# Forgetting attention with each head pair's query tiles in the order 0 1 6 7 2 3 4 5, page probabilities copied first in ScalarE's order, and the first decay rows in two transfers

## The reference, cut to what matters

```python
s = einsum(q_i, k) * 64 ** -0.5 + D[query] - D[key]      # D = cumsum(log f)
s = where(key position <= query position, s, -1e30)
p = softmax(s);  o = p @ v
```

## Time and profile before

| | us |
|---|---|
| median of three runs | 1789.3 |
| the profiled execution, as timed | 1788.96 |
| its span, first to last instruction | 1787.1 |
| forgetting attention, first instruction to the first of the next stage | 455.5 to 639.2 |

### The profile page before, as it was taken

The page is one execution under the profiler, slowest core; times in us unless marked ns, Lnnn a source line. Parts: engine busy times, 40 slices in busy tenths (PEclk is TensorE's granted clock), DMA queues, the critical chain, the costliest instruction groups (busy, mean ns, idle before and its releaser), DMA issues. The chain is left out here.

```text
span 1787.1 us, 27685 instructions
## 1 busy us (share of the span) xinstructions
PE 1568.5 (88%) x10583; PEld 1384.9 (77%) x10587; DVE 1030.4 (58%) x1718; ACT 624.8 (35%) x1112; POOL 744.3 (42%) x837
## 2 busy tenths in 40 slices
PE   4699989999688866999699559999999999699996
PEld 2467879999466645799587459999999999588874
DVE  1461009630455533555424596887777777669885
ACT  2432133231344442223223334443333442444352
POOL 1431014321000007775103469999999996000011
PEclk8899999999799987899699779999999999799998
DMA  8335532220421048422323202222222221885872
GB/s 328 113 138 166 189 108 81 80 87 15 142 63 31 29 140 224 105 84 76 118 104 94 69 24 85 73 79 79 73 73 73 88 83 70 256 292 176 278 243 93
DMA packets 136981, 211.00 MB, mean 118 GB/s; under 512 B 38756, under 2 KB 78484, under 8 KB 133522
## 3 DMA queue, kind: packets, MB, share of 16 engines
q1 hardware_dynamic: 134386, 200.32, 34.7%
q10 hardware_dynamic: 2464, 8.91, 1.3%
HBM read 166.16 MB, written 42.91 MB: 117 GB/s over the span
## 5 line engine op out<-in xcount | busy, mean ns | idle before, releaser
L2701 DVE SCALAR_TENSOR_TENSOR fu_tmp<-fu_zp,fu_cw,fu_tmp 128x1024 f32<-128x1024 f32 x88 | 150.9, 1714 | 75.9 <-ACT fu_tmp L2636 74.3
L2446 PE MATMUL fu_ps<-fu_thi,fu_wlo 128*128 128x272 f32 (+2 forms) x672 | 139.2, 288 | 0.0
L2446 PE MATMUL fu_ps<-fu_tlo,fu_whi 128*128 128x272 f32 (+2 forms) x672 | 138.9, 288 | 0.0
L2446 PE MATMUL fu_ps<-fu_thi,fu_whi 128*128 128x272 f32 (+2 forms) x672 | 138.9, 288 | 0.0
L3023 PE MATMUL fd_ps<-fd_bhi,fd_ahi 128*128 128x512 f32 x308 | 121.3, 394 | 19.2 <-DVE fd_blo L3134 19.2
L2478 POOL TENSOR_TENSOR fu_wlo<-fu_s,fu_whi 128x512 fp32r<-128x512 f32 x84 | 119.6, 1434 | 18.7 <-ACT fu_whi L2592 18.2
L2592 ACT ACTIVATE fu_whi<-fu_s 128x512 fp32r<-128x512 f32 x84 | 50.8, 628 | 216.1 <-PE fu_ps L2446 84.2
L3023 PE MATMUL fd_ps<-fd_blo,fd_ahi 128*128 128x512 f32 x308 | 121.1, 393 | 0.0
L3023 PE MATMUL fd_ps<-fd_bhi,fd_alo 128*128 128x512 f32 x308 | 121.1, 393 | 0.0
L2446 PE MATMUL fu_ps<-h_hi,fu_whi 128*128 128x272 f32 (+1 forms) x504 | 105.6, 291 | 15.4 <-POOL fu_wlo L2478 15.4
L2478 POOL TENSOR_TENSOR fu_wlo<-w_raw,fu_whi 128x512 fp32r<-128x512 f32 x67 | 109.8, 1640 | 9.7 <-ACT fu_whi L2592 9.7
(11 more groups left out here) (398 smaller groups left out, 4000.9 us busy)
## 6 DMA issues: line engine op xcount, KB each, us to landing
wa<-in_w_ada SPq DMA_DIRECT2D x24, 1024.0 KB, 5.6
w_raw<-in_w_up SPq DMA_DIRECT2D x88, 256.0 KB, 2.6
fd_b<-in_w_down SPq DMA_DIRECT2D x86, 256.0 KB, 3.7
fd_a<-scr_y SPq DMA_DIRECT2D x86, 256.0 KB, 3.7
scr_y<-fu_tmp SPq DMA_DIRECT2D x22, 544.0 KB, 4.5
fp_w<-in_w_fm SPq DMA_DIRECT2D x15, 512.0 KB, 3.4
scr_qkv<-fp_y SPq DMA_DIRECT2D x9, 512.0 KB, 2.9
dr_stg<-scr_qkv SPq DMA_DIRECT2D x8, 576.0 KB, 5.8
```

Source lines behind the costliest of these rows:

```text
L2446: last = pe.matmul(lane_of(q, o)[:, n, 0:size], w[:, o, kk], part(low, kk, slice(c, c + size)), start=(kk == 0 and m == 0), stop=(kk == HK ...
L2701: one = dve.scalar_tensor_tensor(yp, a, w, yp, ALU.mult, ALU.add)
```

## The change

A tuple `SPANS = (0, 3, 1, 2)` gives the order of tile pairs, and `tile_of(u)` takes the place of `u % NT` everywhere: a pair's tiles now come in the order 0 1, 6 7, 2 3, 4 5. ScalarE does `spread_c` at the head of its turn u, before `exp(u, 0)`, where it stood after the copies. `decays(0)` becomes four transfers, columns 0 to 255 of both rows with a semaphore of their own, then columns 256 to 1023 of both, and it is issued ahead of the table. Unit 0 waits for the first columns, unit 2 for the rest.

```diff
+        SPANS = (0, 3, 1, 2)
-        nb_in = [sem("fa_nb_in0"), sem("fa_nb_in1")]
+        nb_in, nb_first = [sem("fa_nb_in0"), sem("fa_nb_in1")], sem("fa_nb_first")
+        def tile_of(u):
+            return 2 * SPANS[u % NT // 2] + u % 2
...
         def output(eng, q, hh):
-            j, m = q // (NT // 2), q % (NT // 2)
+            j, m = q // (NT // 2), SPANS[q % (NT // 2)]
...
             def decays(j):
-                for hh in range(2):
-                    after(sp, max_set, 2 * NT * (j - 1))
-                    sp.dma_start(nb[:, j % 2, hh], K.scr_nd[2 * j + hh:2 * j + hh + 1].broadcast_to([P, SEQ])).then_inc(nb_in[j % 2], 16)
+                after(sp, max_set, 2 * NT * (j - 1))
+                for c in (slice(0, QC), slice(QC, SEQ)) if j == 0 else (slice(0, SEQ),):
+                    for hh in range(2):
+                        sp.dma_start(nb[:, j % 2, hh, c], K.scr_nd[2 * j + hh:2 * j + hh + 1, c].broadcast_to([P, c.stop - c.start]))\
+                            .then_inc(nb_first if c.stop == QC else nb_in[j % 2], 16)
...
+            decays(0)
             sp.dma_start(table[:], K.page_table).then_inc(table_in, 16)
-            decays(0)
             sp.wait_ge(table_in, 16)
             pages(0)
             decays(1)
...
             def scores(u):
-                j, i = u // NT, u % NT
+                j, i = u // NT, tile_of(u)
...
             for u in range(UNITS + 2):
+                if (u - FIRST) % 3 == 2 and 0 <= (u - FIRST) // 3 < NBATCH:
+                    spread_c((u - FIRST) // 3)
                 before = mine(u - 1, False) if 0 < u <= UNITS else []
...
                     for n in (before[:half], before[half:])[hh]:
                         spread(act, n)
-                if (u - FIRST) % 3 == 2 and 0 <= (u - FIRST) // 3 < NBATCH:
-                    spread_c((u - FIRST) // 3)
...
             def maximum(u, hh):
-                j, i = u // NT, u % NT
+                j, i = u // NT, tile_of(u)
                 n = (i + 1) * P
-                if i == 0:
+                if u == 0:
+                    dve.wait_ge(nb_first, 32)
+                if u == QC // P or u and u % NT == 0:
                     dve.wait_ge(nb_in[j % 2], 32 * (j // 2 + 1))
```

More of the change, by code:

```diff
@@ L1058, in forgetting_attention @@
             for hh in range(2):
-                for b in range(0, u % NT + 1, 4):
-                    groups.append((u, hh, b, min(4, u % NT + 1 - b)))
+                for b in range(0, tile_of(u) + 1, 4):
+                    groups.append((u, hh, b, min(4, tile_of(u) + 1 - b)))
         group_of = {g[:3]: n for n, g in enumerate(groups)}
@@ L1076, in spread @@
             u, hh, b, size = groups[n]
-            q, i = u // 2, u % NT
+            q, i = u // 2, tile_of(u)
             eng.wait_ge(t_mm, n + 1)
@@ L1234, in exp @@
             def exp(u, hh):
-                n = (u % NT + 1) * P
+                n = (tile_of(u) + 1) * P
                 act.wait_ge(max_set, 2 * u + hh + 1)
@@ L1290, in i_last @@
             def i_last(u):
-                return (u % NT) // 4 * 4
+                return tile_of(u) // 4 * 4
             def scale(u, hh):
```

## The result

The changed kernel takes 1780.55 us (median of 9 runs, 1775.64 to 1784.36) where the kernel before took 1791.4 us beside it (9 runs). The ratio is 0.9931, interval 0.991 to 0.9952: 12.3 us (9 to 16) of 1789.3, against the 12.7 forecast (1789.3 less 1776.6). The profiled execution was timed at 1777.7 us and its span is 1775.6 us, 11.5 less than before. Forgetting attention runs from 455.4 to 628.1 us: 172.7 us long instead of 183.7, so 11.0 of the 11.5 lie in this stage.

The account below looks back on a forecast made before the run. TensorE (88% busy) was taken to carry the kernel, held up by waits on ScalarE's copies and clock falls. Terms -2.0 - 7.4 - 6.3 + 3.1 = -12.6 us gave 1776.6 us, range 1770.5 to 1784.

Parts of the forecast that it names:

- part 3: Split first decay rows, table behind them: 2.85 us gained early, page 0 late; net +3.1 us, bounds -2.0 and +6.
- part 1: New tile order: shorter `turn` stalls, partly returned at new neighbours and before `turn_c(5)`; -2.0 us in sum.
- Part 2: `spread_c` first: copies lie in ScalarE's idle time, so waits before `values_c` go; -7.4 us, bounds -7.4 and -2.
- The clock: Low-clock time after the waits before `values_c` goes with them: -6.3 us, bounds 0 and -7.9.
- no difference: Rival: `spread_c` delays the exponentials (+5), page 0 late (+3), clock as before; 1788 to 1790 us, chance 0.08.
- the fall in part 3: Clock falls after the 3.9 us page wait before `scores_c(0)`: 5.5 us low, 2.5 us lost.
- The fall before `turn_c(5)`: The 2.0 us wait behind `scale_c` may bring a clock fall back; given half of 7 us x 0.46, 1.6 us.
- 6→7: Stall inside `turn` of tile 6 beside tile 7; claimed to stay in the new order.
- the next `turn` stall absorbs: Of the 2.5 us lost to low clock after the page wait, 1.1 us is absorbed by the following `turn` stall.
- page 0 in time: Rival: decay rows do not hold up the table; part 3 gives -2.0 instead of +3.1, 1771.5 us, chance 0.13.
- the clock falls all the same: Rival: waits of 1.66 to 2.0 us keep low-clock time as it was; 6.3 us lost, 1782.9 us, chance 0.22.
- Slower: Rival: after the page wait the clock stays low for the rest of the first pair; 1792 us, chance 0.05.

Follow-up runs that it names:

- e1: Kernel before with only `spread_c` moved to the head of ScalarE's turn: stage 170.0 us against 183.7, ratio 0.9888.
- e5: Changed kernel without the split decay transfers and with the table first; new order and `spread_c` first kept: stage 171.9 us, ratio 0.9927.
- e2: Kernel before with only the new tile order: stage 180.6 us against 183.7, ratio 0.9985.
- the four pairs above: Runs differing in tile order alone, all with `spread_c` first; new order longer: e5 less e1 +1.9 us, e4 less e6 +0.2, e10 less e11 +1.8, e7 less e12 +2.0.
- e4: Changed kernel with the table issued ahead of the four decay transfers: stage 168.0 us against 172.7, ratio 0.9882.
- e3: Kernel before with only the first decay rows split and the table issued behind them: stage 189.1 us against 183.7, ratio 1.002.
- e9: Changed kernel run again, unedited: stage 172.5 us, ratio to the kernel before 0.9905.
- e10: The changed kernel with the table first (e4) run again, unedited: stage 169.5 us, ratio 0.9922.
- e7: Changed kernel with the table first (e4), and VectorE's `scale_c` between the two maxima: stage 168.7 us, ratio 0.9906.
- e8: Changed kernel with the table issued between the first and second pair of decay transfers: stage 170.0 us, ratio 0.9911.
- e6: Changed kernel with the table first (e4), but tiles in the old order: stage 167.8 us, ratio 0.9915.
- e11: The old-order, table-first kernel (e6) run again, unedited: stage 167.7 us, ratio 0.991.
- e12: The old-order, table-first kernel (e6) with `scale_c` between the two maxima: stage 166.7 us, ratio 0.9917.

## Why the prediction was right

The time followed the likeliest case. The part that carries the gain, its mechanism and the times of the loads came out; the prices of the two small parts did not. Taken one after the other, the stage changes by -13.7 us with `spread_c` first (e1), +1.9 with the order added (e5) and +0.8 with part 3 (after). Forecast were -7.4 - 6.3 = -13.7, then -2.0 and +3.1. The last two are off by +3.9 and -2.3 us, and that they partly cancel is luck. So is the match of the first: the forecast's -13.7 holds 1.6 us for a fall of part 1, and e1 its late rise.

- **Part 2, -7.4 of waits.** Right: no wait on the copy is left, and e1 alone gives -13.7 us with the clock. ScalarE's idle time covers the copies; the 5 us of the rival "no difference" didn't come.
- **The clock, -6.3, and the fall in part 3, +2.5.** Net -3.8 was forecast for low-clock time. It went from 17.1 to 10.2 us, x 0.46 = -3.1. The first fall lasted 6.8 us, put at 5.5; 0.9 of it lies inside the page wait and costs nothing, so 5.9 are left, 0.2 us too many at 0.46. The fall before `turn_c(5)`, put down at one half of 7 us, came whole but half as long, in both profiles of the changed kernel: the same 1.6 us, by luck. It was put between "the 1.81 that did not and the 2.33 that did", but the third fall of before had followed a 1.43; the runs show no such threshold (last section).
- **Part 1, -2.0.** Alone it gives -3.1 (e2), beside `spread_c` first +0.2 to +2.0 (the four pairs above). The wait before `turn_c(5)` is 1.97 us (2.0 forecast). The `turn` stalls are 12.9 us in 12 waits, against 11.5 in 11. Timeline of the changed kernel, one stall of each kind that was missed:
```profile
486.30 2.02 PE L1173 MATMUL fa_psT<-fa_dg,fa_p 128*128 128x128 f32 x16 [0.27 <-ACT fa_pt L1090]
513.69 1.58 PE L1173 MATMUL fa_psT<-fa_dg,fa_p 128*128 128x128 f32 x12 [0.57 <-ACT fa_pt L1090]
531.56 1.80 PE L1173 MATMUL fa_psT<-fa_dg,fa_p 128*128 128x128 f32 x14 [1.89 <-ACT fa_pt L1090]
619.66 1.58 PE L1173 MATMUL fa_psT<-fa_dg,fa_p 128*128 128x128 f32 x12 [0.62 <-ACT fa_pt L1090]
```
  Of the 1.4 us, 0.6 is a stall that the sum had at nothing: the last tile of the stage, now tile 5, stalls although no unit follows it. 7→2 comes to 1.1 (0.27, 0.41, 0.41; 0.8 forecast) and 5→0 to 1.0 (0.57, 0.41; 0.7 forecast). 6→7 was carried over at its old 1.69 us ("6→7 stays"): it is 1.89 in unit 11, where `decay_c`, queued ahead of the maxima, lets VectorE start them 0.2 late. In unit 3 it would be 2.6 us (e4, e5), which the page wait hides. A stall depends on what the third engine has queued at that turn, not only on the two neighbouring tiles.
- **Part 3, +3.1.** The mechanism was right in its times: first maximum 458.99 (458.4 forecast), SyncE reads the table from 460.6 on (461.0), first page load 461.65 (462), page 0 complete by 469.98 (470.3). The wait is 2.91 us and not 3.9, mostly because TensorE arrived at 467.07 instead of 466.4; that is no gain, only the page was 0.3 early. The 1.1 us of the fall that "the next `turn` stall absorbs" weren't absorbed: TensorE was back at the higher clock in that `turn`, and the stall at 479.99 is a full 1.69. Two readings were wrong. Loads of 128 KB do stand in the trace of before (`tp_lng`, `tp_lnb`: 9.0 and 8.9 us to landing, and 3.0 for the pair here), and `gpre` was issued behind 3.0 MB, not 3.5. As a term of the sum, 3.1 is no single number: part 3 costs 5.4 us alone (e3), and 0.8 beside the other two (e5), because the long stall of unit 3 and a fall come without it too. Against the table issued first it costs 4.7 (e4) or 3.0 (e9 less e10). What the forecast called "the 2.85 gained are spent, and more" is shown by e4: with the table first the gain of the split stays and the page is in time.
- **The sum.** -12.6 was forecast in the profiled execution. The stage gives -11.0 and ends at 628.1 instead of 626.5; the stages behind it keep their length (1147.9 us before, 1147.5 after). Missing are 1.6. The `turn` stalls hold 1.4, the absorption that didn't come 1.1 and low clock 0.2; against them page 0 was 0.3 early and the waits for `scale_c` grew by 0.9 instead of 1.1. That makes 2.2; the difference of 0.6 is not placed.

Of the rivals, "page 0 in time" fell by the load's issue at 461.65, and "the clock falls all the same" by the 100 us at full clock from 477 on. It was no idle rival, though: e5 has 10.2 us of low clock without any page wait. "Slower" fell, as the fall behind the page wait was over by 477.

## What to carry to other kernels

A copy that another engine waits for belongs at the head of the helper engine's turn as soon as its input is ready; it costs nothing while the helper would be idle there, and in the profiled stage here it saved more by itself (13.7 us) than the whole change did (11.0). A tiny load on which other loads depend is issued ahead of large ones on the same queue (4.7 and 3.0 us of the stage here, not told apart in the whole time). When work is reordered between two engines, look at what a third has queued in each of the new places, and price a part both alone and beside the others.

## What the runs showed of the hardware

- The granted clock (1.2 or 2.4 GHz) falls behind short waits, in a way that one wait's length doesn't fix. In the profiles here, apart from the waits for `spread_c`: behind 2.6 us in unit 3 it fell in e2, e4, e5, e7 and e10, each time; behind the page waits of 2.8 to 3.9 us in the changed kernel, e9 and e3, each time; behind 1.97 us before `turn_c(5)` in the changed kernel, e9, e2, e5 and e8, but not in e4 and e10; behind 1.88 or 1.89 us in unit 11 in e5 and e8, but not in the changed kernel, e4, e7, e9 and e10. In e1, e6, e11 and e12, whose waits behind the rise are 1.8 us or less, never; but in e7 it fell behind 0.71 and 0.58. Waits for `spread_c` of 2.3 to 3.8 us were followed by a fall each time (before, e2, e3), and so were 0.90 and 1.43 us in a row (before, e3). Near the stage's end, e3 and the kernel before have the same two waits, 1.81 and then 0.86 us; the clock fell in e3 (at 619) and stayed up before the change (at 614).
- One fall costs 3.4 or 6.8 us of low-clock time, 1.6 or 3.1 us of time by the earlier trace rows. The third fall before the change cost 3.1, behind waits of 0.90 and 1.43.
- 64 bytes on SyncE's queue were read by SyncE 3.4 us after their own issue with 1 MB issued ahead of them (457.22 to 460.6), 2.4 with 256 KB ahead (e8) and 1.5 with nothing ahead (e5).
